# One gather per expert tile: U and V rows side by side, six ring buffers, a pipeline of single tiles

## The chip, the core and the metric

The kernel runs on one core of a Trainium2 chip. The metric is the device time of one execution in microseconds (us). The median of three runs of the kernel before is 3443.48 us (3442.27 to 3449.14).

## The reference

Two pre-norm residual layers over 256 tokens of width 2048 (f32). The first layer mixes tokens with a bidirectional mLSTM, the second with grouped-query attention. Behind each mixer comes a PEER channel mixer, which the change is about: per token 8 heads pick 16 of 16384 experts each, and every chosen expert costs one row of a table `u` and one row of a table `v`, 2048 floats (8 KB) each.

```
def peer(xn, wq, k1, k2, u, v):
    q = (xn @ wq).reshape(B, S, PEER_HEADS, 2, PEER_HALF)
    s1, s2 = q[..., 0, :] . k1, q[..., 1, :] . k2
    t1, i1 = lax.top_k(s1, 16); t2, i2 = lax.top_k(s2, 16)
    top_s, pos = lax.top_k(all sums t1 + t2, 16)
    idx  = the pair's i1 * 128 + i2;  gate = softmax(top_s)
    act = gelu(einsum('td,ted->te', x_blk, u[i_blk]))
    return einsum('te,ted->td', gate * act, v[i_blk])
```

## The kernel before

One core does all of it in a single program: mLSTM layer, PEER 0, attention layer, PEER 1. The tokens lie on the 128 partitions in two blocks of 128. In PEER the work is cut into 16 units per layer (8 heads for block 0, then 8 heads for block 1), each unit into 16 tiles, k = 0 to 15: tile k holds the k-th expert of every token, so a tile of `u` is 128 rows of 8 KB (1 MB), and so is one of `v`. Two layers have 512 tiles in all.

The engines hand a tile on through semaphores. POOL gathers the U tile into one of 4 slots (`u_slot`, freed when the dot has read it, `u_used`) and the V tile into one of 8 slots (`v_slot`, freed when TensorE has used it, `v_used`), U and V in turn, in one program order. DVE multiplies and sums U with the normed tokens (the "dot"). After four dots (a group; two and then one in a layer's last unit) it prepares the GELU argument for four columns (`pre`), ACT computes the tanh, DVE multiplies with the gate (`post`), and ACT scales the identity matrix with each of the four columns (`diag`, four buffers). PE multiplies each `diag` with the V tile into four PSUM banks, which keep the running sum of a block (`seed` puts the residual in them first).

Beside this runs the router of the later heads: SP loads the 2 MB of query weights of head h (`load_queries`) once the router of head h - 1 is done (`rq_full`), into one pair of buffers; PE computes it in four parts between the tiles of the unit two heads earlier, ACT copies queries and scores out, and DVE does the top-k of the next unit in one piece behind dot 8. The router of head 0 uses two slots of the ring for its weights, so POOL waits for `rq_full` ahead of its fifth V tile; that of head 1 is computed whole ahead of the first tile on PE. The order on each engine is written out by hand, partly in hardware loops (`Fori`).

At the end of PEER 0, SP starts the loads of the attention weights when the last dot is done; at the end of PEER 1 the four banks are copied out and stored.

Of the kernel before, what the change touches and what calls it, by code (L numbers as in the profile page):

```python
# [19 lines left out]
P = 128  # L20
# [66 lines left out]
def trunk_kernel(nc, consts, x, ln_mix, ln_ffn, m_w_in, m_gate_bias, m_head_norm, m_w_out,  # L87
                 a_w_in, a_q_norm, a_k_norm, a_w_out, wq, k1T, k2T, u_tab, v_tab, out):
# [15 lines left out]
    NU, NVS = 4, 8  # L104
# [3 lines left out]
    with ExitStack() as ctx:  # L108
# [22 lines left out]
        ring_sb = sb_placed("ring_sb", (NU + NVS) * SLOT)  # L131
# [14 lines left out]
        ring = [ring_sb[:, s * SLOT:(s + 1) * SLOT] for s in range(NU + NVS)]  # L146
# [7 lines left out]
        actT_lo = parts_in("actT_lo", KT * T, "ring_sb", 10 * SLOT)[:, :].rearrange("p (k t) -> p k t", t=T)  # L154

        w_gate_parts = parts_in("w_gate_parts", 2 * KT * 16, "ring_sb", 9 * SLOT)
        w_gate_hi, w_gate_lo = (w_gate_parts[:, i * KT * 16:(i + 1) * KT * 16] for i in range(2))
        gatesT = ring[8][0:16, 0:T]
# [4 lines left out]
        EXPERTS = u_tab.shape[1]  # L163
        u_rows, v_rows = (t.rearrange("l e d -> (l e) d") for t in (u_tab, v_tab))
# [32 lines left out]
        u_landed = [sem(f"u_landed{s}") for s in range(NU)]  # L197
        v_landed = [sem(f"v_landed{s}") for s in range(NVS)]
        u_used = sem("u_used")
# [10 lines left out]
        m_qkT = ring_sb[:, 8 * SLOT:10 * SLOT].rearrange("p (k t) -> p k t", t=T)  # L210
# [11 lines left out]
        h_junk = ring[8][:, 0:CH]  # L222
# [143 lines left out]
        def _(sp):  # L366
# [45 lines left out]
            sp.wait_ge(u_used, NU + UNITS * TOPK)  # L412
# [14 lines left out]
        def _(pool):  # L427
# [12 lines left out]
            def gathers(l):  # L440
# [5 lines left out]
                def unit(gu, par, first=False):  # L446
                    pool.wait_ge(idx_ready, gu + 1)
                    settle(pool)
                    nc.gpsimd.tensor_copy(idx_cur[par][:, :], idx_next[:, :]).then_inc(idx_taken, 1)  # L449
                    pool.wait_ge(idx_taken, gu + 1)  # L450
                    for k in range(TOPK):
                        pool.wait_ge(u_used, gu * TOPK + (k + 1))
                        settle(pool)
                        nc.gpsimd.indirect_dma_start(  # L454
                            out=u_slot[k % NU], out_offset=None, in_=u_rows,
                            in_offset=bass.IndirectOffsetOnAxis(ap=idx_cur[par][:, k:k + 1], axis=0),
                        ).then_inc(u_landed[k % NU], 16)
                        if first and k == FIRST_QUERY_SLOT:
# [3 lines left out]
                        settle(pool)  # L462
                        nc.gpsimd.indirect_dma_start(  # L463
                            out=v_slot[k % NVS], out_offset=None, in_=v_rows,
                            in_offset=bass.IndirectOffsetOnAxis(ap=idx_cur[par][:, k:k + 1], axis=0),
                        ).then_inc(v_landed[k % NVS], 16)
                        if first and k == 0:
                            norm(2 * l + 1, [1])

                for par in range(2):  # L470
                    unit(l * UNITS + par, par, par == 0)
                with pool.Fori(1, UNITS // 2) as pair:
                    for par in range(2):
                        unit(pair * 2 + (l * UNITS + par), par)
# [1057 lines left out]
```

## Time and profile before

| | us |
|---|---|
| median of 3 runs | 3443.48 |
| the profiled execution's own time | 3454.97 |
| its span, first to last instruction | 3453.2 |
| PE / DVE / POOL / ACT busy | 2891.7 / 1813.0 / 1641.0 / 543.6 |
| mean granted TensorE clock | 0.914 |

The profiled execution is 11.5 us above the median and 1.8 us longer than its own span. Busy times don't add up to the span, since the engines work beside one another; the share of the DMA engines is shown apart, slice by slice.

### The profile page before, as it was taken

How to read it: one execution, taken by the hardware profiler on the slowest of the kernel's cores; microseconds unless marked ns; L12 is line 12 of the kernel's file. 1: busy time of each engine (PE TensorE's matmuls, PEld its weight loads, DVE VectorE, ACT ScalarE, POOL GpSimd, SP SyncE). 2: the span in 40 equal slices, each digit the busy share in tenths (PEclk: the TensorE clock that was granted, in tenths of full speed). 3: DMA queues.
4: the chain of work that ended last, by engine and by line, in shares of the span. 5: the costliest groups of instructions: out<-in, count | busy, mean ns of one | idle time of the engine just before them, and what ended most of it. 6: DMA issues, size and time to landing. Idle time of an engine off the chain costs nothing.

```text
span 3453.2 us, 28521 instructions
## 1 busy us (share of the span) xinstructions
PE 2891.7 (84%) x8488; PEld 1616.0 (47%) x8488; DVE 1813.0 (53%) x3333; ACT 543.6 (16%) x1103; POOL 1641.0 (48%) x1137
## 2 busy tenths in 40 slices
PE   7999978888897877778789998888889778777777
PEld 5877764444443333333337776444444333333333
DVE  3021135555566666556545654555556666666554
ACT  4334310000000100000014441100000010000001
POOL 4667544444455555555521102444445555555552
PEclk9999999999998888888899998999999888888999
DMA  6545369999999999999994436999999999999998
GB/s 214 171 146 170 127 263 419 420 420 420 418 420 420 420 419 419 420 421 420 420 370 158 147 116 240 420 421 420 420 420 421 420 420 420 420 421 421 421 420 347
DMA packets 212126, 1228.73 MB, mean 356 GB/s; under 512 B 21088, under 2 KB 21856, under 8 KB 75744
## 3 DMA queue, kind: packets, MB, share of 16 engines
q0 software_dynamic: 147456, 1073.81, 75.0%
q1 hardware_dynamic: 63888, 148.67, 12.4%
q10 hardware_dynamic: 720, 5.44, 0.4%
q8 instruction: 38, 0.62, 0.1%
q14 instruction: 24, 0.20, 0.0%
HBM read 1225.74 MB, written 2.10 MB: 356 GB/s over the span
## 4 chain that ended last, share of the span: by engine, by line
DMA 38%; PE 28%; issue 16%; POOL 10%; DVE 7%; ACT 1%; POOLq 0%; DVEq 0%; ACTq 0%; SPq 0%
DMA ring_sb<-in_peer_u_dram,idx_cur 37%; PE bank L963 16%; PE bank L791 7%; POOL w_parts L339 6%; PE bank L844 4%; DVE ring_sb L1289 3%; POOL ring_sb L463 3%; POOL ring_sb L454 1%; POOL idx_cur L449 1%; DMA arena<-in_peer_wq_dram 0%; PE bank L768 0%; ACT diag L631 0%; PE bank L1022 0%; PE bank L1052 0%; DVE shared L1135 0%
## 5 line engine op out<-in xcount | busy, mean ns | idle before, releaser
L963 PE MATMUL bank<-ring_sb,diag 128*128 128x512 f32 x4096 | 1939.1, 634 | 465.4 <-ACT diag L631 463.2
L1289 DVE CUSTOM_DVE_ANT_0 ring_sb<-ring_sb,arena 128x2048 f32<-128x2048 f32 x512 | 1169.9, 2294 | 1009.1 <-DMA ring_sb<-in_peer_u_dram,idx_cur 1006.1
L963 PEld LDWEIGHTS bank<-ring_sb,diag 128*128 128x128 f32 x4096 | 824.3, 204 | 1542.0 <-issue 1329.6
L463 POOL DMA_INDIRECT ring_sb<-in_peer_v_dram,idx_cur x512 | 673.7, 1316 | 606.9 <-PE bank L963 427.0
L454 POOL DMA_INDIRECT ring_sb<-in_peer_u_dram,idx_cur x512 | 612.9, 1197 | 663.2 <-DVE shared L1289 496.0
L791 PE MATMUL bank<-w_parts,actT_hi 128*128 128x512 f32 x1664 | 525.8, 398 | 12.1 <-DVE actT_lo L326 9.8
L339 POOL TENSOR_TENSOR w_parts<-ring_sb,w_parts 128x2048 fp32r<-128x2048 f32 x62 | 287.4, 4644 | 157.8 <-ACT w_parts L333 157.7
L791 PEld LDWEIGHTS bank<-w_parts,actT_hi 128*128 128x128 f32 x1664 | 317.8, 192 | 82.6 <-DVE actT_lo L326 11.5
L791 PE MATMUL bank<-w_parts,actT_lo 128*128 128x512 f32 x832 | 329.0, 395 | 0.0
L626 ACT ACTIVATE shared<-shared 128x4 f32<-128x4 f32 (+1 forms) x138 | 28.4, 206 | 1593.6 <-DVE shared L1298 1586.8
L333 ACT CAST w_parts<-ring_sb 128x2048 fp32r<-128x2048 f32 x104 | 198.3, 1909 | 348.5 <-DMA ring_sb<-in_mlstm_w_in_dram 160.1
L631 ACT ACTIVATE diag<-const,shared 128x128 f32<-128x128 f32 x512 | 166.8, 391 | 479.4 <-DVE shared L1306 460.9
L844 PE MATMUL bank<-actT_sb,arena 128*128 128x256 f32 x896 | 201.7, 379 | 1.8 <-DMA arena<-in_peer_wq_dram 1.8
L844 PEld LDWEIGHTS bank<-actT_sb,arena 128*128 128x128 f32 x896 | 170.0, 190 | 45.7 <-issue 22.5
L791 PEld LDWEIGHTS bank<-w_parts,actT_lo 128*128 128x128 f32 x832 | 159.5, 192 | 33.9
L339 DVE TENSOR_TENSOR w_parts<-ring_sb,w_parts 128x2048 fp32r<-128x2048 f32 x42 | 96.0, 2290 | 100.0 <-ACT w_parts L333 100.0
L433 POOL TENSOR_TENSOR small<-small,const 128x1 f32<-128x1 f32 x8 | 4.5, 566 | 174.4 <-DVE small L1072 174.4
L768 PE MATMUL bank<-const,arena 128*128 128x128 f32 x160 | 28.3, 331 | 56.2 <-DVE arena L1075 38.4
L433 POOL TENSOR_TENSOR q_r<-q_ms,const 128x8 f32<-128x8 f32 x5 | 14.5, 2901 | 127.8 <-DVE q_ms L1378 127.8
L449 POOL COPY idx_cur<-idx_next 128x16 uint32<-128x16 uint32 x32 | 45.8, 1432 | 47.8 <-DVE x_sb L1160 24.3
L306 DVE COPY actT_sb<-bank 128x512 f32<-128x512 f32 x10 | 6.9, 692 | 85.9 <-PE bank L929 78.0
L768 PEld LDWEIGHTS bank<-const,arena 128*128 128x128 f32 x160 | 22.3, 169 | 63.2 <-DVE arena L1075 27.6
(158 smaller groups left out, 1110.6 us busy)
## 6 DMA issues: line engine op xcount, KB each, us to landing
ring_sb<-in_mlstm_w_in_dram SPq DMA_DIRECT2D x48, 1024.0 KB, 5.1
arena<-in_peer_wq_dram SPq DMA_DIRECT2D x28, 1024.0 KB
ring_sb<-in_attn_w_in_dram SPq DMA_DIRECT2D x24, 1024.0 KB, 5.1
ring_sb<-in_mlstm_w_out_dram SPq DMA_DIRECT2D x16, 1024.0 KB, 5.1
ring_sb<-in_attn_w_out_dram SPq DMA_DIRECT2D x16, 1024.0 KB, 5.0
ring_sb<-in_peer_u_dram,idx_cur POOLq DMA_INDIRECT x512
ring_sb<-in_peer_v_dram,idx_cur POOLq DMA_INDIRECT x512, 16.5
ring_sb<-in_peer_wq_dram SPq DMA_DIRECT2D x4, 1024.0 KB, 8.2
```

The lines of the kernel that those rows point to most:

```text
L333: nc.scalar.copy(w_hi_of[j], ring[j]).then_inc(w_hi, 1)
L339: ops.tensor_tensor(w_lo_of[j], ring[j], w_hi_of[j].bitcast(F32), ALU.subtract).then_inc(w_lo[j], 1)
L449: nc.gpsimd.tensor_copy(idx_cur[par][:, :], idx_next[:, :]).then_inc(idx_taken, 1)
L454: nc.gpsimd.indirect_dma_start(out=u_slot[k % NU], out_offset=None, in_=u_rows, in_offset=bass.IndirectOffsetOnAxis(ap=idx_cur[par][:, k:k ...
L463: nc.gpsimd.indirect_dma_start(out=v_slot[k % NVS], out_offset=None, in_=v_rows, in_offset=bass.IndirectOffsetOnAxis(ap=idx_cur[par][:, k: ...
L626: nc.scalar.activation(e_th[:, k0:k1], e_in[:, k0:k1], ACT.Tanh, scale=GELU_C).then_inc(tanh_out, 1)
L631: nc.scalar.activation(diag[k % 4][:, :], ident, ACT.Copy, scale=e_w[:, k:k + 1]).then_inc(diag_ready, 1)
L768: last = tp(trb[at % 2][:, i * P:(i + 1) * P], src[:, f * P:(f + 1) * P], ident)
L791: last = mm(acc[2 * par + b][:, :], xp, wp, start=(j == 0 and k == 0 and i == 0), stop=(j == 3 and k == QK - 1 and i == 2), skip_group_che ...
L844: last = mm(mis[0][:, side * T + t0:side * T + t1], slots[half][:, k % 8, side * P:(side + 1) * P], actT[:, k, t0:t1], start=(k == 0), sto ...
L963: last = mm(acc[n][:, :], diag[k % 4][:, :], v_slot[k % NVS][:, n * CH:(n + 1) * CH], start=False, stop=end and k == TOPK - 1, skip_group_ ...
L1289: v.tensor_tensor_reduce(u_slot[k % NU], u_slot[k % NU], xn[b], 1.0, 0.0, ALU.mult, ALU.add, dots[:, k:k + 1]).then_inc(u_used, 1)
```

## The change

The two tables become one, `uv_tab`, whose row holds an expert's U row and behind it its V row (16 KB); the host lays it out so. One gather brings both into one of six slots of two old slots each (`uv_slot`), with a semaphore each (`uv_landed`), and a slot is freed only when PE is done with it (`v_used`). Each tile is finished alone: its dot, two small DVE operations, tanh of one column on ACT, one more small DVE operation ahead of the tanh's result and one behind it, and one `diag` of six. The top-k of the next unit is cut in three pieces (`side_top`, `pair_top`, `chosen`), behind tiles 4, 7 and 10. The router parts stand ahead of tiles 0, 2, 4 and 6 instead of 2, 4, 6 and 8, and ACT copies queries behind tile 9 and scores behind tile 14. The hardware loops over units are written out. Buffers of the other stages that lie in the ring move to other slots, and SP's wait ahead of the attention weights is for PE's use of tile 253 of 256 instead of the last dot.

```
-    NU, NVS = 4, 8
+    NUV = NDIAG = 6
...
+        uv_slot = [ring_sb[:, 2 * i * SLOT:(2 * i + 2) * SLOT] for i in range(NUV)]
+        u_slot, v_slot = ring[0::2], ring[1::2]
+        LAYER_TILES = UNITS * TOPK
...
+        FIRST_QUERY_SLOT = 5
+        wq0_slot = [ring[2 * FIRST_QUERY_SLOT + i].rearrange("p (k n) -> p k n", n=2 * P) for i in range(2)]
...
+        VALUES_AT, PAIRS_AT, CHOSEN_AT = 4, 7, 10
+        QUERY_AT = {0: 0, 2: 1, 4: 2, 6: 3}
+        QUERY_COPY_AT, SCORES_AT, SCORES_COPY_AT = 9, 11, 14
...
-            sp.wait_ge(u_used, NU + UNITS * TOPK)
+            sp.wait_ge(v_used, NUV + LAYER_TILES - 2)
...
(POOL)
                     for k in range(TOPK):
-                        pool.wait_ge(u_used, gu * TOPK + (k + 1))
-                        settle(pool)
-                        nc.gpsimd.indirect_dma_start(
-                            out=u_slot[k % NU], out_offset=None, in_=u_rows,
...
-                        ).then_inc(u_landed[k % NU], 16)
+                        if u == 0 and k == FIRST_QUERY_SLOT:
                             pool.wait_ge(rq_full, l * (HEADS + 1) + 2)
                         pool.wait_ge(v_used, gu * TOPK + (k + 1))
+                        at = slot_of(gu, k)
                         nc.gpsimd.indirect_dma_start(
-                            out=v_slot[k % NVS], out_offset=None, in_=v_rows,
+                            out=uv_slot[at], out_offset=None, in_=uv_rows,
...
(PE)
                     for k in range(TOPK):
-                        if k in (2, 4, 6, 8) and head is not None:
-                            router(l, head, parts=[ROUTER_PARTS[k // 2 - 1]])
+                        if head is not None and k in QUERY_AT:
+                            router(l, head, parts=[ROUTER_PARTS[QUERY_AT[k]]])
...
(DVE)
+                    def expert(k):
+
+                        at, c = slot_of(gu, k), slice(k, k + 1)
+                        dve.wait_ge(uv_landed[at], 16 * uses(gu, k))
+                        v.tensor_tensor_reduce(u_slot[at], u_slot[at], xn[b], 1.0, 0.0, ALU.mult, ALU.add,
+                                               dots[:, c]).then_inc(dot_done, 1)
+                        dve.wait_ge(dot_done, gu * TOPK + k + 1)
+                        need(did(v.scalar_tensor_tensor(out=e_t[:, c], in0=dots[:, c], scalar=GELU_A, in1=dots[:, c],
+                                                        op0=ALU.mult, op1=ALU.mult)))
+                        v.scalar_tensor_tensor(out=e_in[:, c], in0=e_t[:, c], scalar=1.0, in1=dots[:, c],
+                                               op0=ALU.add, op1=ALU.mult).then_inc(tanh_in, 1)
+                        need(did(v.tensor_tensor(e_p[:, c], dots[:, c], gate_cur[:, c], ALU.mult)))
+                        dve.wait_ge(tanh_out, gu * TOPK + k + 1)
+                        v.scalar_tensor_tensor(out=e_w[:, c], in0=e_th[:, c], scalar=1.0, in1=e_p[:, c],
+                                               op0=ALU.add, op1=ALU.mult).then_inc(w_ready, 1)
```

On PE at the start of a layer's PEER, from the router of head 1 (32 matmuls from `arena`) and its scores (`keysT`) to the first tiles (`ring_sb,diag`, four matmuls a tile), the program of before reads:

```order
L844 MATMUL bank<-actT_sb,arena 128x256 [waits wq_landed1]
L844 MATMUL bank<-actT_sb,arena 128x256 x23
L856 MATMUL bank<-keysT,shared 128x128 [waits rq_out]
L856 MATMUL bank<-keysT,shared 128x128 x3
L976 UNCONDITIONAL_BRANCH
L976 ISA
L961 ISA [waits diag_ready]
L963 MATMUL bank<-ring_sb,diag 128x512 [waits v_landed0]
L963 MATMUL bank<-ring_sb,diag 128x512 x3
```

and that of the change at the same place:

```order
L839 MATMUL bank<-actT_sb,arena 128x256 [waits wq_landed1]
L839 MATMUL bank<-actT_sb,arena 128x256 x23
L851 MATMUL bank<-keysT,shared 128x128 [waits rq_out]
L851 MATMUL bank<-keysT,shared 128x128 x3
L839 MATMUL bank<-actT_sb,arena 128x256 [waits wq_landed0]
L839 MATMUL bank<-actT_sb,arena 128x256 x7
L962 MATMUL bank<-ring_sb,diag 128x512 [waits uv_landed0,diag_ready]
L962 MATMUL bank<-ring_sb,diag 128x512 x3
L962 MATMUL bank<-ring_sb,diag 128x512 [waits uv_landed1,diag_ready]
L962 MATMUL bank<-ring_sb,diag 128x512 x3
```

The first router part of head 2, with its wait for that head's query weights, has moved ahead of the layer's first tile.

On DVE, in the first unit, before (the ISA rows of L1289 are the dot and the reading of its sum):

```order
L1289 ISA ring_sb,shared<-ring_sb,arena 128x2048 [waits u_landed3]
L1289 ISA shared 128x1
L1295 ISA
L1296 TENSOR_TENSOR shared<-shared 128x4 [waits u_used]
L84 REGISTER_ALU
L1297 TENSOR_SCALAR shared<-shared 128x4 [waits dve_done]
L84 REGISTER_ALU
L1298 TENSOR_TENSOR shared<-shared 128x4 [waits dve_done]
L1288 REGISTER_ALU
L1289 ISA ring_sb,shared<-ring_sb,arena 128x2048 [waits u_landed0]
L1289 ISA shared 128x1
L1303 REGISTER_ALU
```

and with the change:

```order
L1294 ISA ring_sb,shared<-ring_sb,arena 128x2048 [waits uv_landed0,dve_done]
L1294 ISA shared 128x1
L1297 SCALAR_TENSOR_TENSOR shared<-shared 128x1 [waits dot_done]
L1299 SCALAR_TENSOR_TENSOR shared<-shared 128x1 [waits dve_done]
L1301 TENSOR_TENSOR shared<-shared 128x1
L1303 SCALAR_TENSOR_TENSOR shared<-shared 128x1 [waits tanh_out,dve_done]
L1294 ISA ring_sb,shared<-ring_sb,arena 128x2048 [waits uv_landed1]
```

The wait for ACT's tanh stands behind each dot instead of behind the fifth.

On POOL, where a layer's gathers begin, before:

```order
L454 DMA ring_sb<-in_peer_u_dram,idx_cur 128x2048 [waits u_used]
L463 DMA ring_sb<-in_peer_v_dram,idx_cur 128x2048 [waits rq_full,v_used]
L454 DMA ring_sb<-in_peer_u_dram,idx_cur 128x2048 [waits u_used]
L463 DMA ring_sb<-in_peer_v_dram,idx_cur 128x2048 [waits v_used]
L454 DMA ring_sb<-in_peer_u_dram,idx_cur 128x2048 [waits u_used]
```

and with the change:

```order
L460 COPY idx_cur<-idx_next 128x16 [waits idx_ready,w_used]
L467 DMA ring_sb<-in_peer_uv_dram,idx_cur 128x4096 [waits v_used,idx_taken]
L467 DMA ring_sb<-in_peer_uv_dram,idx_cur 128x4096 [waits v_used] x4
L467 DMA ring_sb<-in_peer_uv_dram,idx_cur 128x4096 [waits v_used,rq_full]
L467 DMA ring_sb<-in_peer_uv_dram,idx_cur 128x4096 [waits v_used] x10
```

Every gather now waits for `v_used`. Counted over all five engines, the written-out program lists 12033 instructions where that of before lists 6297.

## Rows read from the trace of the kernel before

**Rows 1.** The page: the span in 40 slices.
```profile
PE   7999978888897877778789998888889778777777
DMA  6545369999999999999994436999999999999998
GB/s 214 171 146 170 127 263 419 420 420 420 418 420 420 420 419 419 420 421 420 420 370 158 147 116 240 420 421 420 420 420 421 420 420 420 420 421 421 421 420 347
```
**Rows 2.** Windows of a PEER stage: busy by engine, clock, DMA share, GB/s.
```profile
900.00:1000.00 100.00, 88.00 (x241) 45.34 (x240) 55.53 (x103) 9.87 (x30) 50.06 (x41) 0.93 1.01 419
1100.00:1200.00 100.00, 82.73 (x168) 34.91 (x168) 58.13 (x104) 12.28 (x33) 51.96 (x41) 0.88 1.01 420
3410.00:3420.00 10.00, 7.15 (x18) 2.98 (x17) 5.33 (x9) 0.93 (x4) 3.76 (x4) 1.00 1.01 421
```
**Rows 3.** Windows of the first 24 us, where SP's first weights land.
```profile
10.00:14.00 4.00, 1.94 (x8) 1.57 (x8) 1.66 (x2) 2.00 (x2) 0.14 (x1) 1.00 1.01 391
20.00:24.00 4.00, 2.55 (x10) 2.05 (x9) 1.58 (x3) 2.93 (x3) 0.00 (x0) 1.00 1.04 386
```
**Rows 4.** The page: DMA queues, and two DMA issues (KB each, us to landing).
```profile
q0 software_dynamic: 147456, 1073.81, 75.0%
q10 hardware_dynamic: 720, 5.44, 0.4%
q8 instruction: 38, 0.62, 0.1%
...
ring_sb<-in_mlstm_w_in_dram SPq DMA_DIRECT2D x48, 1024.0 KB, 5.1
shared<-in_consts_dram ACTq DMA_DIRECT2D x1, 1216.0 KB, 8.7
```
**Rows 5.** Windows at the start of PEER 0's gathers.
```profile
460.00:480.00 20.00, 9.18 (x68) 8.13 (x66) 9.07 (x39) 4.43 (x7) 2.68 (x4) 0.87 0.05 9
480.00:500.00 20.00, 16.64 (x88) 13.99 (x89) 10.62 (x10) 1.54 (x3) 13.90 (x9) 0.71 0.99 396
```
**Rows 6.** The timeline there: start, us, operation, idle before it.
```profile
477.22 1.17 POOL L454 DMA_INDIRECT ring_sb<-in_peer_u_dram,idx_cur  x1 [0.99 <-POOL idx_cur L449]
500.47 13.98 PE L844 MATMUL bank<-actT_sb,arena 128*128 128x256 f32 x64
514.63 0.87 SPq L392 DMA_DIRECT2D arena<-in_peer_wq_dram  x2
516.85 0.21 ACT L626 ACTIVATE shared<-shared 128x4 f32<-128x4 f32 x1
518.10 7.13 PE L963 MATMUL bank<-ring_sb,diag 128*128 128x512 f32 x16 [1.82 <-ACT diag L631]
522.61 0.94 POOL L463 DMA_INDIRECT ring_sb<-in_peer_v_dram,idx_cur  x1 [11.30 <-DVE shared L1289]
527.05 3.72 PE L844 MATMUL bank<-actT_sb,arena 128*128 128x256 f32 x16 [1.82 <-DMA arena<-in_peer_wq_dram]
```
**Rows 7.** The timeline at the end of PEER 1: the last tile.
```profile
3435.64 14.00 PE L963 MATMUL bank<-ring_sb,diag 128*128 128x512 f32 x32 [3.42 <-ACT diag L631]
3436.98 2.29 DVE L1289 CUSTOM_DVE_ANT_0 ring_sb<-ring_sb,arena 128x2048 f32<-128x2048 f32 x1 [0.63 <-DMA ring_sb<-in_peer_u_dram,idx_cur]
3439.89 0.20 ACT L626 ACTIVATE shared<-shared 128x1 f32<-128x1 f32 x1 [3.10 <-DVE shared L1298]
3440.51 0.40 ACT L631 ACTIVATE diag<-const,shared 128x128 f32<-128x128 f32 x1 [0.42 <-DVE shared L1306]
3449.68 0.59 ACT L642 COPY x_sb<-bank 128x512 f32<-128x512 f32 x1 [0.27 <-PE bank L963]
```
**Rows 8.** The timeline at the end of PEER 0: its last dot and matmuls.
```profile
1794.17 2.29 DVE L1289 CUSTOM_DVE_ANT_0 ring_sb<-ring_sb,arena 128x2048 f32<-128x2048 f32 x1 [0.62 <-DMA ring_sb<-in_peer_u_dram,idx_cur]
1792.83 17.04 PE L963 MATMUL bank<-ring_sb,diag 128*128 128x512 f32 x32 [2.71 <-ACT diag L631]
```
**Rows 9.** The timeline of a unit: the top-k's ends, and a gather beside a dot.
```profile
1041.57 0.29 DVE L1087 COPY shared<-arena 128x256 f32 x1
1050.33 2.28 DVE L1289 CUSTOM_DVE_ANT_0 ring_sb<-ring_sb,arena 128x2048 f32<-128x2048 f32 x1
1004.41 2.71 POOL L463 DMA_INDIRECT ring_sb<-in_peer_v_dram,idx_cur  x1 [1.05 <-PE bank L963]
```

More of the change, by code:

```diff
@@ L145, in trunk_kernel @@
         actT = actT_sb[:, :].rearrange("p (k t) -> p k t", t=T)
-        ring = [ring_sb[:, s * SLOT:(s + 1) * SLOT] for s in range(NU + NVS)]
+        ring = [ring_sb[:, s * SLOT:(s + 1) * SLOT] for s in range(RING)]
         w_parts = parts_in("w_parts", 8 * SLOT, "ring_sb")
@@ L196, in trunk_kernel @@
         top_ready, gexp_ready, idx_ready, idx_taken = (sem(n) for n in ("top_ready", "gexp_ready", "idx_ready", "idx_taken"))
[L197 to L199 removed]
+        uv_landed = [sem(f"uv_landed{s}") for s in range(NUV)]
+        dot_done = sem("dot_done")
         v_used = sem("v_used")
@@ L444, in gathers @@
                     pool.wait_ge(acc_out, 4 + 2 * ALL_CHUNKS)
-                def unit(gu, par, first=False):
+                for u in range(UNITS):
+                    gu, par = l * UNITS + u, u % 2
                     pool.wait_ge(idx_ready, gu + 1)
-                    settle(pool)
                     nc.gpsimd.tensor_copy(idx_cur[par][:, :], idx_next[:, :]).then_inc(idx_taken, 1)
@@ L659, in peer @@
                     load_gain(3)
-                with act.Fori(0, HEADS - 2) as h:
-                    unit(h + base, True, head=h + 2)
-                unit(base + HEADS - 2, True)
-                unit(base + HEADS - 1, True)
+                for u in range(HEADS):
+                    unit(u)
                 results(0)
@@ L666, in peer @@
                     square(2, 0)
-                with act.Fori(0, HEADS - 1) as h:
-                    unit(h + (base + HEADS), True)
-                unit(base + UNITS - 1, False, LAST_GROUPS)
+                for u in range(HEADS, UNITS):
+                    unit(u)
                 results(1)
@@ L975, in peer @@
                 router_scores(l, 1)
-                with pe.Fori(0, HEADS - 2) as h:
-                    unit(h + base, False, head=h + 2)
-                unit(base + HEADS - 2, False)
-                unit(base + HEADS - 1, True)
+                for u in range(HEADS):
+                    unit(u)
                 pe.wait_ge(x_out, 4 * (NB * l + 1))
                 seed(1)
-                with pe.Fori(0, HEADS - 1) as h:
-                    unit(h + (base + HEADS), False)
-                unit(base + UNITS - 1, True)
+                for u in range(HEADS, UNITS):
+                    unit(u)
             peer(0)
@@ L1348, in _ @@
+                for u in range(UNITS):
+                    unit(u)
             peer(0)
             norm(2, 0, 3)
+            dve.wait_ge(v_used, NUV + LAYER_TILES)
             lo_groups(dve, "n2", range(0, 2))
```

188 lines of the change are left out of this document (72 added, 116 removed).

## The prediction

> **What bounds the kernel now.** I read the slices first. In two stretches, from slice 7 to 20 and from slice 26 to 39, the DMA engines stand at 9 tenths or more and move 420 GB/s without a dent [rows 1]; these are the two PEER stages. The windows say the same at finer grain: DMA share 1.01 and 419 to 421 GB/s, while PE is busy 83 to 88%, DVE about 57% and POOL about 51% [rows 2]. So inside PEER the DMA engines are the bound, and every other engine waits for them. All 1073.8 MB of gathers go through queue 0 [rows 4]: at 420 GB/s they take 1.048576 / 420 = 2.497 us per MB, 4.99 us per pair of U and V tile, 2557 us of the whole. The change moves the same bytes. It can therefore only act in three ways: what a byte costs on the DMA engines, whether they ever run dry, and what stands ahead of the first and behind the last transfer of a stage.
>
> **Cost of a byte.** The 128 rows of 1 MB go as 8 packets to each of 16 engines, plus one for the completion (147456 = 1024 x 144 packets, [rows 4]). With 16 KB rows there are half as many. The trace has no 16 KB gather, so I bound it. From one side, nothing is gained if a packet's time only follows its bytes: 0 us. From the other, the two windows at the start hold SP's first weight loads, of 2 KB rows (512 columns of a matrix), with the DMA engines full: 391 GB/s, or 386 [rows 3]. Per engine a packet of 2 KB takes 16 x 2048 / 391 = 83.8 ns, and one of 8 KB takes 16 x 8192 / 420 = 312.1 ns. The line through both has 7.7 ns that no byte pays for (9.1 ns with 386). A tile saves 8 such costs per engine, 62 to 73 ns, and 512 tiles save 32 to 37 us. That rows longer than 8 KB stay one packet is seen on queue 10: its 720 packets are five transfers of 144, and one of them is the constants' table, 1216 KB or 9.5 KB a row [rows 4]. I take -34 us; a packet of 2 KB and one of 8 KB are the nearest rows, and 0 stays an end of the range.
>
> By the Trainium skill, page "DMA: Bandwidth & Descriptors", section "Bandwidth", a packet costs about 3 cycles inside the DMA engine above its bytes, which at the 850 MHz that it gives is 3.5 ns, under half of what the windows show. The saving would then be an estimated 512 x 8 x 3.5 ns = 14 us. The windows are this kernel's own and I go by them.
>
> **Running dry in the steady stretch.** Six slots at 4.92 us are 29.5 us. A slot's way round: landing, dot 2.29, then from the dot's end (3439.28) to the end of `diag` (3440.91) 1.7 us in the one single tile that the trace shows [rows 7], then 8 matmuls in 7.13 / 2 = 3.6 us [rows 6], then POOL's gather, 0.94 us or up to 2.7 us where a dot stands beside it [rows 6, 9], and about 2 us more until its data moves. That is 7.6 us on the engines and some 5 us to the next data, against the 24.6 us that the other five tiles take: 12 us to spare. DVE holds a tile for 2.29 + 0.9 = 3.2 us, and the top-k, now in three pieces, costs 1050.33 - 1041.57 = 8.8 us a unit [rows 9]: 16 x 3.2 + 8.8 = 60 us of 79. PE needs 16 x 3.6 + 4 x 3.7 + 1.2 = 73.6 us in a unit with router [rows 6] (1.2 us for the scores, 8 small matmuls), and the DMA engines 16 x 4.92 + 5 = 83.7 us, since those units also carry 2 MB of query weights. The tile-by-tile rhythm leaves PE idle 1.4 us in 5; in the pair rhythm, with 2.9 us gaps at the same share of work (7.15 of 10 us), the granted clock is 1.00, the 2.4 GHz level [rows 2]. Cost: 0, hidden behind the DMA engines.
>
> **The start of a PEER stage.** This is where the change pays. Before, 17 MB are in flight or landed before POOL must wait for a matmul: U tiles need only a dot, V tiles have 8 slots. POOL then stands 11.3 us at the ninth V tile and goes on at 522.61, and the stream still holds [rows 6]. With the change it is six tiles, 12 MB. Data starts at about 480: the share is 0.05 in 460 to 480 and 0.99 behind it [rows 5]. The 12 MB end at 480 + 12 x 2.46 + 1.2 (the slower first window, 396 GB/s) = 511. The seventh gather needs PE to be done with tile 0, and PE now has the first router part of head 2 ahead of it. Its weights are issued at 514.63, when the router of head 1 is done [rows 6]; a 1 MB load into a quiet queue lands 5.1 us later [rows 4], at 519.7. The part takes 3.7 us, the tile 3.6: 527.0. `diag` 0 is no hindrance, since the tanh can start at 516.85. From the gather's start to data the first one takes 480 - 477.2 = 2.8 us [rows 5, 6]: data at about 530. From 511 to 530 the DMA engines have only the query weights (5.0 us) and, in PEER 0, one gain vector of 1 MB (2.5 us) to move: 11.5 us dry in PEER 0, 14 in PEER 1, which starts in the same rhythm. PE then goes through its backlog of tiles and router parts, 10.9 us for each two tiles with a part against 9.8 us of DMA, and opens three or four more holes of 0.5 to 1.5 us: 2 us a stage. Sum +29.5 us; from 0 (if the seventh gather came in time) to +37 (a gather beside a dot, 2 us each; PE at its lower clock after the wait, 3.7 us more for one part).
>
> **The end of a stage.** Call T the end of the last transfer, some 2.5 us behind the landing of the last U tile before: 3439.5 and 1796.7 [rows 7, 8]. Before, the last 32 matmuls start when the third-last tile's weight is ready and run 14.00 and 17.04 us, to T + 10.1 and T + 13.2. With the change only tile 255 is left: dot 2.3, chain 1.7, matmuls 3.6: T + 7.6. That is -2.5 and -5.6; at the lower clock in the last tile it would be +1 and -2.2. I take -6.5 for both. SP's new wait comes true about 2 us before T, and the attention weights still queue right behind the last gather: 0. The boundary from block 0 to 1 holds PE for four copies and 8 matmuls, some 7 us, within the 12 us to spare: 0.
>
> **Instructions.** Twice the listed instructions, so about another 0.6 MB like that of queue 8 [rows 4], 1.5 us at 420 GB/s, in stages where DMA is the bound: +1.5 us. Fewer POOL instructions (512 gathers for 1024) buy nothing, since POOL is waited for nowhere in the steady stretch.
>
> **Sum.** -34 + 29.5 - 6.5 + 1.5 = -9.5 us. The profiled execution of 3454.97 us would take 3445.5; on the median of 3443.48 that is 3434.0 us.
>
> **Rivals.**
> - *The larger packet buys little or nothing.* For it: the 2 KB rows may be slow for another reason, such as reading short pieces of wide rows. The sum is then +24.5 us, 3468 us, and +10.5 or 3454 with the saving halved and a little less; it decides below 27 us of saving. The rule of the Trainium skill above is this rival, by an estimated 14 us. Chance 0.22.
> - *The start doesn't run dry*, because PE or SP come earlier than I count. The sum is -39 us, 3404.5 us. Against it stand the wait in the listing and 514.63. Chance 0.10.
> - *PE becomes the bound in the units with a router.* 73.6 us at full clock against 83.7: the point is a mean granted clock of 0.88, and exactly that was granted over long stretches before [rows 2]. At 0.85 a unit takes 86.6 us, 2.9 more, and 12 units 35 us: the sum is +25, 3469 us. For it: a granted clock of 0.88 to 0.93 with work in long bursts. Against it: the shorter gaps. Chance 0.13.
>
> **How the numbers follow.** The forecast has 0.55, with its own range of 3420 to 3447. The range over all, 3407 to 3467, leaves out about half of the no-gain case and of the PE case and most of the early start, together 0.2. A measurement of this kernel can tell about 0.2%, 6.9 us, from no change. Of the forecast's 0.55, 0.33 lies beyond that on the fast side, 0.20 inside and 0.02 beyond on the slow side. Faster: 0.33 + 0.10 = 0.43. Same: 0.20 + 0.02 = 0.22. Slower: 0.02 + 0.20 + 0.13 = 0.35.
>
> **What would show it.** In the windows of a steady stretch, GB/s rises from 420 to 425 or 426 (right), or stays at 420 (the first rival). In the 50 us behind a stage's first gather, POOL's seventh gather starts 48 to 50 us behind the first, released by PE, and the DMA share falls well under 1 between 30 and 50 us (right), or it doesn't (second). In units with a router, a DMA share under 1.00 beside PE at 9 tenths or more is the third. At the end, PE's last matmuls come 7.6 us behind the last landing. The forecast is wrong above all if the size of a packet doesn't matter or if a hole opens once a unit, which I count at nothing: 1 us a unit would be 32 us.

## The result and the profile after

The changed kernel takes 3452.41 us (median of 9 runs, 3448.66 to 3455.98) against 3443.48 before (9 runs): a ratio of 1.0025 [1.0014, 1.0035]. It is slower by 9 us, a quarter of a per cent, where 9.5 us less were forecast. Its profiled execution has a span of 3450.5 us at a mean granted clock of 0.967.

The span of before is longer (3453.2), which would read as a gain. The two spans must be cut first: outside PEER that execution of before was slower (first gather at 477.22 [rows 6], in the changed kernel at 471.63). From a stage's first gather to its last copy, before took 1332.7 and 1327.7 us, the changed kernel 1334.0 and 1334.4: 8 us more, as the medians say.

The page of the changed kernel, the slices that answer to [rows 1], and its queues:

```profile
PE   7999979888887777777779997988888777777777
DMA  6545469999999999999985435899999999999997
GB/s 214 171 147 170 137 250 378 427 426 427 426 426 428 426 426 427 423 423 419 425 353 171 134 134 233 371 427 427 426 427 427 426 427 426 425 427 414 427 418 334
...
q0 software_dynamic: 73728, 1073.77, 73.6%
...
q8 instruction: 67, 1.10, 0.1%
q14 instruction: 67, 0.54, 0.0%
```

The steady slices rose from 420 GB/s to 426 and 427. But the first slice of each stage has 378 and 371 where before has 419 and 420, a few late ones dip, and the last has 334 for 347. Queue 8 had 38 packets before [rows 4]; queue 14 stands in the page of before as

```profile
q14 instruction: 24, 0.20, 0.0%
```

Windows of the steady stretch, as [rows 2]:

```profile
900.00:1000.00 100.00, 87.40 (x241) 43.85 (x242) 68.09 (x166) 13.67 (x45) 23.59 (x22) 1.00 1.01 427
1100.00:1200.00 100.00, 77.00 (x167) 30.82 (x167) 68.48 (x178) 16.72 (x48) 22.30 (x20) 0.98 1.01 426
```

The DMA engines are still full and PE's clock is 1.00 and 0.98 for 0.93 and 0.88: PE is no bound. Windows at the start of PEER 0, and the timeline there, as [rows 6]:

```profile
500.00:510.00 10.00, 9.32 (x45) 7.92 (x44) 0.00 (x0) 0.58 (x1) 0.00 (x0) 1.00 0.36 152
510.00:520.00 10.00, 6.45 (x26) 5.22 (x25) 7.68 (x14) 2.30 (x7) 0.00 (x0) 0.83 0.83 316
520.00:530.00 10.00, 10.00 (x32) 5.89 (x31) 9.13 (x35) 1.21 (x4) 1.89 (x2) 1.00 0.53 200
```
```profile
471.63 1.17 POOL L467 DMA_INDIRECT ring_sb<-in_peer_uv_dram,idx_cur  x1 [0.70 <-POOL idx_cur L460]
495.01 13.98 PE L839 MATMUL bank<-actT_sb,arena 128*128 128x256 f32 x64
514.37 5.16 PE L839 MATMUL bank<-actT_sb,arena 128*128 128x256 f32 x16 [3.55 <-DMA arena<-in_peer_wq_dram]
519.37 7.03 PE L962 MATMUL bank<-ring_sb,diag 128*128 128x512 f32 x16
523.24 0.94 POOL L467 DMA_INDIRECT ring_sb<-in_peer_uv_dram,idx_cur  x1 [30.73 <-PE bank L962]
```

POOL stands 30.73 us at the seventh gather, which comes 51.6 us behind the first. PE gets to tile 0 only behind the router of head 1 (13.98 us), a wait of 3.55 us for the next weights and a router part. Meanwhile the DMA engines are at 0.36 and then 0.53. And the end of PEER 1, windows and then the timeline, as [rows 7]:

```profile
3426.00:3430.00 4.00, 2.80 (x7) 1.03 (x6) 1.95 (x7) 0.60 (x2) 0.00 (x0) 1.00 0.69 291
3430.00:3434.00 4.00, 2.81 (x7) 1.06 (x6) 2.68 (x6) 0.60 (x2) 0.00 (x0) 1.00 0.06 25
3434.00:3438.00 4.00, 3.21 (x8) 1.14 (x6) 2.85 (x6) 0.24 (x2) 0.00 (x0) 1.00 0.07 29
```
```profile
3434.75 2.29 DVE L1294 CUSTOM_DVE_ANT_0 ring_sb<-ring_sb,arena 128x2048 f32<-128x2048 f32 x1 [1.73 <-DMA ring_sb<-in_peer_uv_dram,idx_cur]
3439.64 2.29 DVE L1294 CUSTOM_DVE_ANT_0 ring_sb<-ring_sb,arena 128x2048 f32<-128x2048 f32 x1 [1.71 <-DMA ring_sb<-in_peer_uv_dram,idx_cur]
3443.32 3.70 PE L962 MATMUL bank<-ring_sb,diag 128*128 128x512 f32 x8 [1.20 <-ACT diag L627]
3447.05 0.59 ACT L640 COPY x_sb<-bank 128x512 f32<-128x512 f32 x1 [0.27 <-PE bank L962]
```

The last dot is followed by the last copy within 7.4 us, as forecast. What nobody had forecast stands above it: for some 10 us the DMA share is 0.06, one engine in sixteen, 25 GB/s for 426. Fifteen engines are done, and one still works off its part of the last two tiles at 4.9 us each. PEER 0 ends alike (1790 to 1794: 0.06, 25 GB/s). Before, the stream stays at 420 GB/s until 3434:

```profile
3430.00:3434.00 4.00, 2.22 (x6) 0.67 (x4) 2.00 (x1) 0.16 (x1) 0.00 (x0) 1.00 1.01 420
3434.00:3438.00 4.00, 2.36 (x6) 1.17 (x7) 2.35 (x10) 1.19 (x4) 0.00 (x0) 1.00 0.44 182
```

To size the parts I summed the trace's packet records (start, duration, bytes of each packet) in bins of 10 us. The undisturbed rate is the one that the best quarter of a stage's bins reaches; the 426 GB/s of the windows is a mean that has small holes in it. "Lost" is the time, in us, by which a stretch falls short of the undisturbed rate:

| | undisturbed GB/s | lost in the first 100 us, PEER 0 / 1 | lost behind that |
|---|---|---|---|
| before | 420.5 | 2.3 / 2.1 | 4.6 / 3.3 |
| after | 427.7 | 18.5 / 19.4 | 16.3 / 16.2 |

The balance of the forecast and of the traces, in us over both stages:

| term | forecast | traces |
|---|---|---|
| packets of 16 KB: the changed kernel's two stages less those of a, told below (1073.8 MB at 427.7 for 420.5 GB/s give -43) | -34 | -42 |
| start of a stage: lost in the first 100 us | +29.5 | +33.5 |
| behind the last transfer (first gather to last copy, less the transfers between) | -6.5 | -8 |
| instructions: lost behind the first 100 us (that this is their doing is shown under i to l) | +1.5 | +24.5 |
| sum | -9.5 | +8 |

### The profile page after: what moved, and what is told of

Read it like the earlier page. It is cut to its first block, busy times and chain, and to the rows that moved or that the text cites. A ratio compares the mean times of both kernels' runs of the same rounds, so it can differ in the third digit from the quotient of the medians.

```text
span 3450.5 us, 26730 instructions
## 1 busy us (share of the span) xinstructions
PE 2874.5 (83%) x8488; PEld 1561.9 (45%) x8488; DVE 1986.6 (58%) x4691; ACT 655.0 (19%) x1477; POOL 919.1 (27%) x625
## 3 DMA queue, kind: packets, MB, share of 16 engines
q1 hardware_dynamic: 63888, 148.67, 12.3%
## 4 chain that ended last, share of the span: by engine, by line
DMA 47%; PE 27%; DVE 10%; issue 8%; POOL 6%; ACT 2%; POOLq 0%; DVEq 0%; SPq 0%
DMA ring_sb<-in_peer_uv_dram,idx_cur 46%; PE bank L962 14%; PE bank L786 6%; POOL w_parts L350 6%; DVE ring_sb L1294 6%; PE bank L839 5%; ACT diag L627 1%; ACT shared L624 1%; DVE shared L1299 0%; DVE shared L1297 0%; DVE shared L1303 0%; PE bank L763 0%; PE bank L1048 0%; DMA arena<-in_peer_wq_dram 0%; PE bank L1018 0%
## 5 line engine op out<-in xcount | busy, mean ns | idle before, releaser
L962 PEld LDWEIGHTS bank<-ring_sb,diag 128*128 128x128 f32 x4096 | 774.3, 196 | 1592.2 <-issue 818.1
L467 POOL DMA_INDIRECT ring_sb<-in_peer_uv_dram,idx_cur x512 | 604.3, 1180 | 1919.2 <-PE bank L962 1873.3
L624 ACT ACTIVATE shared<-shared 128x1 f32<-128x1 f32 x512 | 103.8, 203 | 2045.8 <-DVE shared L1299 2045.8
L627 ACT ACTIVATE diag<-const,shared 128x128 f32<-128x128 f32 x512 | 205.5, 401 | 154.2 <-DVE shared L1303 153.0
L1303 DVE SCALAR_TENSOR_TENSOR shared<-shared 128x1 f32<-128x1 f32 x512 | 81.8, 160 | 196.6 <-ACT shared L624 196.6
L1299 DVE SCALAR_TENSOR_TENSOR shared<-shared 128x1 f32<-128x1 f32 x512 | 81.5, 159 | 17.8
L1297 DVE SCALAR_TENSOR_TENSOR shared<-shared 128x1 f32<-128x1 f32 x512 | 81.4, 159 | 17.7
L1301 DVE TENSOR_TENSOR shared<-shared 128x1 f32<-128x1 f32 x512 | 78.6, 154 | 0.0
L1161 DVE TENSOR_TENSOR x_sb<-bank,x_sb 128x512 f32<-128x512 f32 x16 | 10.7, 686 | 75.2 <-PE bank L786 75.2
```

The lines of the kernel that those rows point to most:

```text
L467: nc.gpsimd.indirect_dma_start(out=uv_slot[at], out_offset=None, in_=uv_rows, in_offset=bass.IndirectOffsetOnAxis(ap=idx_cur[par][:, k:k + ...
L624: nc.scalar.activation(e_th[:, k:k + 1], e_in[:, k:k + 1], ACT.Tanh, scale=GELU_C).then_inc(tanh_out, 1)
L627: nc.scalar.activation(diag[slot_of(gu, k)][:, :], ident, ACT.Copy, scale=e_w[:, k:k + 1]).then_inc(diag_ready, 1)
L962: last = mm(acc[n][:, :], diag[slot_of(gu, k)][:, :], v_slot[at][:, n * CH:(n + 1) * CH], start=False, stop=end and k == TOPK - 1, skip_gr ...
L1297: need(did(v.scalar_tensor_tensor(out=e_t[:, c], in0=dots[:, c], scalar=GELU_A, in1=dots[:, c], op0=ALU.mult, op1=ALU.mult)))
L1299: v.scalar_tensor_tensor(out=e_in[:, c], in0=e_t[:, c], scalar=1.0, in1=dots[:, c], op0=ALU.add, op1=ALU.mult).then_inc(tanh_in, 1)
```

## The experiments

Medians, with the ratio to the kernel before run beside it; the last columns are from one trace each: first to last gather packet of each stage, and the packets of 8 KB that carry DVE's instructions (told under i). Letters follow the labels.

| kernel | median us | ratio | stage, PEER 0 / 1 | DVE packets |
|---|---|---|---|---|
| before | 3443.5 | | 1316.8 / 1314.9 | 4 / 4 |
| after | 3452.4 | 1.0025 [1.0014, 1.0035] | 1323.6 / 1324.1 | 21 / 20 |
| a two 8 KB gathers | 3494.9 | 1.0149 [1.0131, 1.0166] | 1344.6 / 1345.0 | 20 / 20 |
| b router parts later | 3438.9 | 0.9986 [0.9976, 0.9996] | 1316.9 / 1315.7 | 19 / 20 |
| c before, PEER written out | 3457.8 | 1.0042 [1.0027, 1.0056] | 1323.3 / 1322.2 | 13 / 12 |
| d start spread out | 3429.6 | 0.9956 [0.9940, 0.9971] | 1311.1 / 1312.1 | 19 / 20 |
| e PE rolled up | 3455.1 | 1.0039 [1.0025, 1.0053] | 1324.7 / 1324.5 | 20 / 19 |
| f DVE rolled up | 3472.9 | 1.0093 [1.0079, 1.0107] | 1333.9 / 1334.0 | 30 / 32 |
| g d, second unit too | 3422.1 | 0.9947 [0.9933, 0.9960] | 1307.4 / 1307.8 | 20 / 20 |
| h g, rolled up | 3444.6 | 1.0009 [1.0000, 1.0018] | 1320.0 / 1322.7 | 31 / 33 |
| i DVE padded | 3488.5 | 1.0132 [1.0112, 1.0152] | 1339.0 / 1339.6 | 37 / 35 |
| j ACT padded | 3450.5 | 1.0024 [1.0015, 1.0033] | 1322.8 / 1322.7 | 24 / 20 |
| k g, less on DVE | 3414.2 | 0.9919 [0.9905, 0.9934] | 1304.0 / 1303.6 | 16 / 16 |
| l k, still less | 3407.1 | 0.9897 [0.9883, 0.9910] | 1299.9 / 1300.7 | 12 / 13 |

**a. Two gathers of 8 KB.**

```
-    nc.gpsimd.indirect_dma_start(out=uv_slot[at], in_=uv_rows, ...).then_inc(uv_landed[at], 16)
+    for dst, rows in ((u_slot[at], u_rows), (v_slot[at], v_rows)):
+        nc.gpsimd.indirect_dma_start(out=dst, in_=rows, ...).then_inc(uv_landed[at], 16)
```

> The change, but with each tile gathered by two gathers of 8 KB rows from the two old tables into the two halves of its slot; all else as changed. If the size of a packet is what lifted the steady rate from 420 to 426 GB/s, the rate falls back to 420, a tile takes 4.99 us again instead of 4.90, and the time rises by 38 to 44 us over the changed kernel, to about 3493 us. If the rate came from elsewhere (gathers that no longer wait beside the dots, the order of the ring), it stays at 426 and the time at 3450 to 3455.

3494.94 us, 42.5 more than the changed kernel. A window of the steady stretch:

```profile
1100.00:1200.00 100.00, 78.69 (x169) 31.46 (x168) 66.36 (x172) 16.72 (x48) 48.05 (x41) 0.97 1.01 420
```

With everything else as in the changed kernel, the rate is back at 420 GB/s. The size of the packet is what raised it. The two stages are 21.0 and 20.9 us longer, at nearly the same losses behind the first 100 us (16.5 and 16.8 us) and the same number of DVE's packets: the larger packet is worth 42 us, not 34.

**b. Router parts where they stood before.**

```
-        QUERY_AT = {0: 0, 2: 1, 4: 2, 6: 3}
+        QUERY_AT = {2: 0, 4: 1, 6: 2, 8: 3}
```

> The change, with the router parts back ahead of tiles 2, 4, 6 and 8. If the dry stretch at a stage's start comes from the first tile's wait for the query weights of head 2, the seventh gather starts about 7 us earlier, each start loses 7 to 9 us less, and the time is 3435 to 3440 us. If six slots alone are the cause (12 MB in flight and PE busy with the router of head 1 until then), little changes: 3448 to 3453.

3438.88 us, 13.5 less than the changed kernel; the first 100 us lose 11.3 and 10.7 for 18.5 and 19.4. So the router part ahead of tile 0 was worth nearly half of the hole, and this one line turns a slower kernel into one a little faster than before.

**c. The kernel before with its PEER loops written out.**

```
-    with pe.Fori(0, HEADS - 2) as h:
-        unit(h + base, False, head=h + 2)
+    for h in range(HEADS - 2):
+        unit(h + base, False, head=h + 2)
```

(and so for every loop over units on POOL, ACT, PE and DVE).

> The kernel before with only its loops over PEER units written out (10813 listed instructions for 6297; 12033 in the change). If fetching instructions loads one DMA engine of the sixteen, which then falls behind the others by some 10 us until the end of each stage instead of 3, the time rises by 9 to 13 us, to 3452 to 3456, and both stages end with a stretch in which the DMA share is 0.06. If the fetched bytes spread over all engines, it is +1 us: 3443 to 3445.

3457.84 us, 15 more. The same operations in the same order cost 6.5 and 7.3 us more a stage once they are written out. That is somewhat more than the 9 to 13 expected. On the page the instruction queues have grown, and later in a stage most slices stand at 414 to 419 GB/s instead of 420; a window of the steady stretch has 417:

```profile
q8 instruction: 67, 1.10, 0.1%
q14 instruction: 57, 0.47, 0.0%
```
```profile
1100.00:1200.00 100.00, 82.50 (x168) 34.83 (x168) 58.01 (x103) 12.16 (x33) 52.34 (x41) 0.87 1.01 417
```

But a long stretch of 25 GB/s at the end did not show here (3.3 and 3.6 us lost in the last 20, for 3.2 and 2.8 before); the loss lies in small holes inside the stage. That the bytes cost something was now shown. How, was not.

**d. The start spread out.** Head 1's router in parts ahead of tiles 2 to 5, head 2's ahead of 10, 11, 13 and 15, the first unit's top-k later.

```
-                router(l, 1)
-                router_scores(l, 1)
+        FIRST_PARTS = {2: (1, 0), 3: (1, 1), 4: (1, 2), 5: (1, 3), 10: (2, 0), 11: (2, 1), 13: (2, 2), 15: (2, 3)}
```

> The change with another order in the first unit of a stage: the router of head 1 no longer stands ahead of the first tile but in four parts ahead of tiles 2 to 5, that of head 2 ahead of tiles 10, 11, 13 and 15, and the top-k of the next unit behind tiles 10, 11 and 12. If the dry starts are 18 us a stage and come from PE being kept from its first tile, they vanish: about -35 us, 3415 to 3420, below the kernel before. If the lost time at the start is only shifted (PE's backlog opens the holes later), it is 3435 to 3450.

3429.57 us, 22.8 less than the changed kernel. The first 100 us lose 1.2 and 2.0: the hole is closed. But not all of it is won, for PE now stands a unit later, at the first router part of head 3, whose weights are loaded only when head 2 is done:

```profile
590.92 5.25 PE L849 MATMUL bank<-actT_sb,arena 128*128 128x256 f32 x15 [7.34 <-DMA arena<-in_peer_wq_dram]
```

This costs 5.1 and 5.0 us between 100 and 150 us behind the first gather.

**e and f. Which instructions?** The same kernel as after, with the 16 written-out units rolled up in threes (48 tiles come back to the same slots), in e on PE alone, in f on DVE alone.

```
+                with pe.Fori(0, 2) as g:
+                    for u in range(3):
+                        unit(u, g)
```

> The changed kernel with PE's unit loops rolled up again in threes (48 tiles come back to the same slots): 10 written-out units instead of 16 on PE alone, 4773 PE instructions for 5505; nothing else is changed. Theory: queue 8 carries PE's instructions (38 packets of 16 KB before, 67 in every kernel with PE written out, however long the others' code is) on one DMA engine of 16, and that engine falls behind in the stage: 22 packets by 0.614 us = 13.5 us, against 7 packets or 4.3 us before. Here some 14 packets, 8.6 us: 4 to 5 us less a stage, 3443 us, 9 less than the changed kernel, and a shorter stretch of 25 GB/s at the end of each stage. Rival A, the bytes are spread over the 16 engines: under 1 us, 3452. Rival B, the last stretch is not from instructions but from 16 KB packets running uneven: 3452 and the stretch stays.

> The changed kernel with DVE's unit loops rolled up in threes (units 1 to 6 and 8 to 13 of a stage; 3785 DVE instructions for 4405), PE left written out. Theory of one engine a queue, with queue 8 the slowest (13.5 us a stage) and DVE's code on queue 14 (29 packets of 8 KB a stage, 9.1 us, on another engine): queue 14 loses some 8 packets, which are not what is waited for: 0 to -1 us, 3452. Rival B1, both queues share one engine: 2.5 us a stage less, 3447. Rival A, spread: 3452 as well.

Both came out otherwise: e 3455.06 us, no gain, and f 3472.85 us, 20 more. The queues, first of e and then of f:

```profile
q8 instruction: 51, 0.84, 0.1%
q14 instruction: 66, 0.54, 0.0%
```
```profile
q8 instruction: 67, 1.10, 0.1%
q14 instruction: 90, 0.73, 0.1%
```

That queue 8 carries PE's code is right: 16 packets fewer. They bought nothing, so queue 8 is not what the stage waits for. In f a body of three units is not kept, so nothing is saved, and its waits on computed counts need instructions of their own: queue 14 rose from 67 to 90 packets, and each stage by 10 us. So the theory of queue 8 had fallen; queue 14 moved with the time. DVE also stood 5.8 us at each jump back:

```profile
DVE shared L1294 <- issue: 11.4, 2, 5.8
```

so f alone could not say whether packets or jumps cost the 10 us.

**g. The second unit's parts two tiles later.**

```
-    if u and head is not None and k in QUERY_AT:
+    if u and head is not None and k - 2 * (u == 1) in QUERY_AT:
```

> The kernel with the repaired start, and in unit 1 the four router parts two tiles later (2, 4, 6, 8 instead of 0, 2, 4, 6). With the repaired start the packet records showed a second hole 110 to 150 us behind the first gather, 5.6 and 4.9 us: PE stood 7.34 us at tile 0 of unit 1 for the weights of head 3, which are issued only when head 2 is done. If these holes go, 9 to 10 us less than the repaired start's 3429.6: 3420. If the hole only moves, 3429.

3422.11 us, 7.5 less than d. The second hole is gone (between its first 100 and its last 20 us a stage loses 8.2 and 9.4 us for 11.6 and 12.4).

**h. g with DVE rolled up, and PE in block 1.**

> The one before with DVE rolled up in threes and PE rolled in block 1 only (13 written-out units for 16, 5242 PE instructions). Theory of PE's queue: some 3 packets of 16 KB fewer a stage, 1.8 us each stage, 3 to 4 us less than the kernel before: 3416. Rivals: spread bytes, no difference, 3420; both queues on one engine, 3411.

3444.59 us, 22.5 more than g instead of less. DVE's packets rose here too, by 11 and 13 a stage.

**What one packet does.** The packet records around one of them in the changed kernel (start in ns by the trace's own clock, duration in ns, bytes):

```
1080225   325    8192   queue 14, instructions
1080538  1273   16384   queue 0, the gather's next packet on that engine (else 614)
```

An engine that fetches instructions loses 0.325 + 1.273 - 0.614 = 0.98 us. On an engine whose packets follow one another without a gap this can be followed: from one such packet to the next, that engine's completions fall back by 1.0 us against the other fifteen, and the difference stays. (Before, with gather packets of 312 ns, the one behind the fetch takes 968 ns: 0.325 + 0.968 - 0.312, the same 0.98 us.) Queue 14 has two kinds, one with 1273 ns beside it (some 20 a stage) and one with 961 to 989 ns (some 7). That the first are DVE's and the second ACT's, each on one DMA engine of its own, was the theory for the next two. A few packets a stage have a gather beside them that fits neither time (2 to 5, in f, h and i 5 to 13), so the counts of DVE's packets are good to some units, j's 24 among them. All 8 KB packets of queue 14 together are 29 and 29 a stage in the changed kernel, and 45 and 45 both in i and in j.

**i and j. The same 2048 instructions a stage, once on DVE and once on ACT.**

```
+        def padding(eng):
+            for i in range(8):
+                eng.sem_inc(pad[i % 4], 1)
...
                     for k in range(TOPK):
                         expert(k)
+                        padding(dve)
```

(in j `padding(act)` behind `diag`).

> The changed kernel with 8 instructions more on DVE behind every tile's chain, each of which only counts up a semaphore that nobody reads: 2048 a stage, by 64 bytes 16 packets of 8 KB. New theory, from the packet records: DVE's instructions come in 8 KB packets through queue 14, always over the same one DMA engine; while one passes, the gather beside it takes 1.27 us instead of 0.614, and that engine falls 0.98 us behind the other fifteen for good. A stage of the changed kernel has 19 or 20 of them (before: 4; before written out: 11; two 8 KB gathers: 18), and it ends with this engine, 10 us behind the rest. Here 35: 16 x 0.98 = 15.7 us a stage, 31 in all, 3484. Rival A, the engines even out and only the bytes count: 16 x 0.98 / 16 = 1 us a stage, 3454. Rival B, the loss is DVE's time: 8 x 0.03 to 0.06 us a tile, hidden in the 1.7 us that DVE waits a tile: 3452 to 3456.

> The same 8 instructions a tile, but on ACT behind diag instead of on DVE. Theory of one DMA engine for each instruction stream: queue 14's other packets (9 or 10 a stage, beside which a gather takes 0.96 to 0.99 us) are ACT's and lie on another engine; with 16 more, some 25, that one falls about as far behind as DVE's: 0 to 5 us a stage, 3452 to 3462, and clearly less than the same instructions cost on DVE. Rival, all of queue 14 shares one engine: as on DVE, 3484. Rival, only bytes count: 3454.

i took 3488.52 us, 36.1 more than the changed kernel, and j 3450.52, none more. In both the page has the same row for queue 14, 98 packets for 67:

```profile
q14 instruction: 98, 0.80, 0.1%
```

In i it is the kind with 1273 ns that grew, 37 and 35 for 21 and 20, and the stages by 15.4 and 15.5 us: 0.96 and 1.03 us a packet. It is not DVE's own time: between 900 and 1780 us DVE still waits 192 us for gathers (in the changed kernel 222). In j it is the other kind, 21 and 23 for 7 and 7, and the stages did not grow. The windows of j's last 10 us show the two engines one after the other:

```profile
3427.00:3430.00 3.00, 2.06 (x5) 0.57 (x3) 2.43 (x6) 0.40 (x2) 0.00 (x0) 1.00 0.13 52
3430.00:3433.00 3.00, 2.74 (x7) 1.31 (x8) 1.51 (x1) 0.21 (x1) 0.00 (x0) 1.00 0.10 44
3433.00:3435.00 2.00, 0.96 (x3) 0.13 (x1) 1.34 (x6) 0.49 (x2) 0.00 (x0) 1.00 0.06 25
```

First two engines of sixteen are behind (0.13, 52 GB/s), then one. (ACT's packets cost less each: 0.309 + 0.989 - 0.614 = 0.68 us, so that some 24 of them stay just short of DVE's 20.) (5 us of i's 36 lie outside the two stages and are not explained.)

**k. Less for DVE.** The tanh's argument is moved to ACT: the dot is scaled by the tanh's constant, and ACT takes Square, then Tanh with the dot as scale and bias.

```
-    v.scalar_tensor_tensor(out=e_t[:, c], in0=dots[:, c], scalar=GELU_A, ...)
-    v.scalar_tensor_tensor(out=e_in[:, c], in0=e_t[:, c], scalar=1.0, ...).then_inc(tanh_in, 1)
+    nc.scalar.activation(e_t[:, k:k + 1], dots[:, k:k + 1], ACT.Square, scale=GELU_A ** 0.5 / GELU_C)
+    nc.scalar.activation(e_th[:, k:k + 1], e_t[:, k:k + 1], ACT.Tanh, scale=dots[:, k:k + 1], bias=dots[:, k:k + 1])
```

> The kernel with both repairs of the start (3422.1), with the square of the dot and the tanh's argument moved to ACT: the dot is scaled by the tanh's constant, ACT takes Square and then Tanh with the dot as scale and as bias; DVE has 2 instructions a tile less (3177 listed for 4201), ACT one more. By the theory DVE's packets fall from 19 or 20 to about 15 a stage, ACT's rise from 9 to 11: 4 to 5 us less a stage, 8 to 10 less in all, 3413, and the stretch of 25 GB/s at the end shortens from 9 or 10 us to 5. Rivals that give DVE's code no part in it: 3420 to 3423 (the last chain is some 0.3 us shorter). If ACT had to load a table between Square and Tanh, each tile would cost it over a microsecond, still inside its 4.9: a longer chain, 3425.

3414.15 us, 8 less than g. 4 packets fewer a stage, and the stages 3.4 and 4.2 us shorter. The end still has its stretch at 0.06; what went are the holes in the middle (5.3 and 5.2 us for 8.2 and 9.4), so of the two signs that were expected this one did not come.

**l. And the product with the gate on ACT.**

```
-    need(did(v.tensor_tensor(e_p[:, c], dots[:, c], gate_cur[:, c], ALU.mult)))
+    nc.scalar.activation(e_p[:, k:k + 1], dots[:, k:k + 1], ACT.Copy, scale=gate_cur[:, k:k + 1]).then_inc(tanh_out, 1)
```

> The kernel before (3414.2) with the product of dot and gate moved to ACT too: one DVE instruction a tile less (2602 listed for 3165), one ACT instruction more. Theory: DVE's packets with a gather of 1.27 us beside them fall from 16 to 13 or 14 a stage, ACT's with 0.98 us rise from 11 to 13 and so stay below: 2 to 3 us less a stage, 4 to 6 in all, 3409. If ACT's engine is the slowest from here on, or PE's, nothing more is won: 3414. If ACT's longer chain (four instructions before diag) mattered, 3416 or more.

3407.08 us: 7 less than k, 45 less than the changed kernel, and 1.0% faster than before. 4 and 3 packets fewer, stages 4.1 and 2.9 us shorter. ACT is busier than it was and is waited for nowhere in the steady stretch:

```profile
1100.00:1200.00 100.00, 81.15 (x174) 32.62 (x172) 60.22 (x106) 26.39 (x90) 25.00 (x21) 0.97 1.01 427
```

Set against one another, each pair a change of DVE's packets with the rest held: c less before, 9 and 8 packets, 6.5 and 7.3 us; i less after, 16 and 15, 15.4 and 15.5; f less after, 9 and 12, 10.3 and 9.9; h less g, 11 and 13, 12.6 and 14.9; k less g, -4, -3.4 and -4.2; l less k, -4 and -3, -4.1 and -2.9. All lie between 0.7 and 1.15 us a packet. In f this leaves nothing for the jumps. What a stage loses behind its first 100 us, at the undisturbed rates, goes the same way over all kernels without a second hole:

| DVE packets a stage | lost, PEER 0 / 1, us | kernel |
|---|---|---|
| 4 | 4.6 / 3.3 | before |
| 12 and 13 | 10.3 / 9.5 and 10.0 / 9.0 | c and l |
| 16 | 13.9 / 13.4 | k |
| 19 to 21 (j: 24 and 20) | 16.2 to 17.5 | after, a, b, e, g, j |
| 30 to 33 | 27.5 / 28.8 and 29.7 / 31.0 | f and h |
| 35 to 37 | 34.0 / 34.0 | i |

**Which engine a fetch falls on.** Each DMA engine completes its part of a tile with a packet of 4 bytes, so its lag can be read tile by tile where nothing else disturbs the stream. In l, from 740 to 900 us behind the first gather packet of the second stage, the sixteen engines keep their distances but for six steps. The two packets of DVE each set the same engine back, by 0.98 and 0.97 us. The two of ACT set back another, also the same both times, by 0.69 and 0.67 us. The two of PE (16 KB, queue 8) set back two different engines, by 1.55 us each. That agrees with e, where 7 to 9 of PE's packets fewer a stage bought nothing: DVE's add up on one engine, and PE's do not.

## Why the prediction was wrong, step by step

- **Cost of a byte: the mechanism right, the size 8 us short.** -34 was taken from the slope between 2 KB and 8 KB packets, and -42 came; a shows that it is the packet. A tile's 8 fewer packets saved 42 / 512 = 0.082 us, 10.3 ns each, against 7.7 forecast. The Trainium skill's 3 cycles (page "DMA: Bandwidth & Descriptors", section "Bandwidth"), an estimated 3.5 ns, are a third of that; here the windows at the start of the trace were the better guide. The first rival falls.
- **Running dry in the steady stretch: the rhythm right, the room left over not.** DVE still waits for the DMA 1.7 us a tile, PE is idle 1.2 us, the clock is 1.00, so PE is no bound and the third rival falls. But the 12 us to spare were counted for sixteen engines in step. They are not: the one that lags takes 10 us of them, and small holes come late in a stage (up to 1.8 us in 10). The last 20 us lose 10.0 and 9.0 us in the changed kernel and no more in i (10.4 and 9.6); what 16 more packets cost there shows as holes in the middle (23.6 and 24.3 us for 6.3 and 7.2). That the fifteen fast engines run ahead only as far as there are free slots would explain both; this was argued, no run varied the slots.
- **The start: right in kind, 4 us short.** The seventh gather came 51.6 us behind the first (48 to 50 forecast), held by PE, with a router part ahead; b and d show both causes. The wait for the weights was 3.55 us, and the part took 5.16 us instead of 3.7.
- **The end: right.** 7.4 us from the last dot's start to the last copy's, and -8 for -6.5 in all.
- **Instructions: the step that failed.** "Twice the listed instructions, so about another 0.6 MB like that of queue 8, 1.5 us at 420 GB/s." The bytes were nearly right (0.82 MB more on queues 8 and 14), the divisor was wrong. They don't spread over sixteen engines. DVE's all lie on one, a fetch of 8 KB costs it 0.98 us, and every tile lands when the last engine has its part. 16 more such packets a stage are 15.7 us on that engine; 12.3 us a stage showed in the changed kernel. With 24.5 for 1.5 the sum goes from -9.5 to +13.5; the start's 4 us more, the packets' 8 us less and the end's 1.5 us less bring it to +8. This one term turns the sign; the error in the packets went the other way and hid 8 us of it. The size of the code grew where it costs because DVE's loops over units, which need not be fetched again (4 packets a stage before, 12 or 13 once written out in c), were written out, with six DVE instructions a tile.

The Trainium skill, page "Runtime: NRT & Kernel Launch", has two accounts of the fetch. Section "The launch sequence" gives it a port of its own; section "Instruction fetch mechanics" has each engine's sequencer fetch through a DMA queue of its own, at a cost that is mostly hidden. The page of this profile lists the fetches as packets on the DMA queues 8 and 14, as the second has it, and they are hidden in j but not in i, where the gathers pay for them; the measurement decides.

What stays open: 16 packets at 0.98 us would be 15.7 us a stage from before to the changed kernel, and 12.3 showed. Some fetches fall into the dry stretch at the start, where they cost nothing; whether that is all of it was not measured. Query weights and missing packet records disturb the stream, so that the engines could be followed for some 100 to 200 us at a time only; that DVE's packets keep to one engine over a whole stage follows from how the losses add up, not from having followed it.

## What to carry to other kernels

Where gathers or loads keep the DMA engines full, written-out code is traffic too: look at the instruction queues of the page, and price each packet of DVE or ACT as 0.7 to 1 us on one engine, not as bytes over sixteen. The busiest code on one engine decides, so take instructions off that engine or give them to one with less code; rolling loops up helps only if the body is small and its counts need no arithmetic. And a DMA share of one sixteenth at the end of a stage says that one engine lags, which no average over the stage shows.

## What was unexpected of the hardware

- The DMA engines don't even out under a full ring: where they can be followed, over some 100 us, a delay of 1 us on one stays.
- DVE's packets fall on one DMA engine, ACT's on another, and PE's on a different one each time (l, 740 to 900 us into the second stage).
- 8 instructions a tile that only count up a semaphore, 2048 a stage, took 16 packets of 8 KB (64 bytes each), and cost 31 us in the two stages on DVE and nothing on ACT.
- A jump back over a long DVE body stood 5.8 us until code came, and with the engines as they were it was hidden.
- Square, Tanh and Copy on ACT one behind the other in every tile cost no visible reload: ACT was busy 26.4 us in 100.
